# The filter stage of a hybrid diffusion step: sine network in halves, fp32r taps, conditioning tiles and P/Q sums on other engines

## The chip, the cores and the metric

The kernel runs on one core of a Trainium2 chip. The time is the device time of one execution in microseconds (us); the figure that counts is the median of several runs. A core has five engines that run side by side and wait for one another on semaphores: TensorE (PE in the profile; PEld are its weight loads), VectorE (DVE), ScalarE (ACT), GpSimd (POOL) and SyncE (SP), which here only issues DMA transfers. Each engine executes its own instructions in order.

## What is computed

One inference step of a two-layer backbone with 1024 latent and 256 context tokens (`TOK` = 1280) and D = 1024. Layer 0 mixes tokens with a bidirectional long convolution, layer 1 with neighbourhood attention; each is followed by a feed-forward block. The change concerns the filters of layer 0 and the first two of the six conditioning vectors:

```python
def ada_params(cvec, w, b):
    m = (jax.nn.silu(cvec) @ w + b)[:, None, :]
    return jnp.split(m, 6, axis=-1)

def hyena_filters(L, pe_w1, pe_b1, pe_w2, pe_b2, pe_w3, sin_freq, decay):
    ...
    hdn = jnp.sin(sin_freq[0] * (feats @ pe_w1 + pe_b1))
    hdn = jnp.sin(sin_freq[1] * (hdn @ pe_w2 + pe_b2))
    k = (hdn @ pe_w3).astype(jnp.float32) * (jnp.exp(-t * jnp.abs(decay)) + MOD_SHIFT)
    return k[:, :D_MODEL], k[:, D_MODEL:]
```

`bidir_long_conv` then places forward and backward taps on a circle (the backward tap of index 0 is not used) and convolves by a Fourier transform. Everything is float32.

## The kernel before

The filter stage comes first. It has a prologue and forty transforms.

The **sine network** runs over all 1280 tokens at once: TensorE multiplies the 33 position features by `pe_w1` in fp32 into a PSUM tile (L709), VectorE applies bias and frequency and reduces the phase to +-pi in six operations (L527 to L541), ScalarE takes the sine (L454). The second layer (L715, the same six operations, L457) does the same with `pe_w2` and 64 rows. ScalarE then copies the first 128 columns of each token part into `hdb`, and VectorE clears its first column (L544), so that the backward taps of index 0 become zero.

The **taps** are made in 40 groups g: ten blocks of 128 tokens for each of four quarters q of 256 channels. `taps(g)` is two fp32 matmuls of 256 columns (L682, L683) with 64 rows. Meanwhile ScalarE makes the window exp(-t|decay|) (`window`, L423). `generate(g)` on VectorE multiplies both (L553, `ker_ok`) and forms forward + backward and forward - backward, P and Q, with two 256-wide operations (L557, L558, `pq_ok`). ScalarE rounds P/Q to the high part of a split in fp32r (`pq_high`, L432), GpSimd subtracts it for the low part (`pq_low`, L377, `pl_ok`). All of `win`, `pq` and the PSUM banks of the taps have two buffers, so that `window(g)` waits for the sums of g - 2 and `generate(g)` for the low part of g - 2.

A **transform** s = 10 q + j multiplies a slice j of the Fourier basis by ten P/Q blocks: 24 fp32r matmuls of 256 columns for j = 0 to 7, 6 for j = 8 and 9 (L702), into one of three banks. The basis is split like the weights, during quarter 0: ScalarE rounds (`basis_hi`, L413), GpSimd subtracts (`basis_lo`, L372). ScalarE copies the odd half of the bank (`odd_half`, L438), VectorE combines it with the even one into `gout` (`combine`, L567 to L571, `spec_ev`), and SyncE stores it to `spec`. While quarter q is transformed the groups of q + 1 are made: three before the first transform, one before each of the next seven (`made_in`). A transform with j = 0 waits for all ten low parts of its quarter.

The **conditioning**: 16 tiles of 128 outputs times two vectors, on TensorE (`early_tile`, L670: 8 blocks of 128x128 fp32 weights against 2 columns). Four stand between the layers of the sine network, the other twelve in pairs behind tap groups 1 to 6. VectorE adds the bias at transform 20 into `mod`. The later conditioning tiles are made on VectorE, where a tile and a vector take one multiply-and-reduce over 1024 columns (L618, L1948, called a row product below).

In quarter 3 no taps are made. The tiles of x are loaded, modulated and split (`x_high`, L447, `x_low`, L578, L583, L396), and the input projection's first two weight entries are split.

SyncE's queue holds, in this order: the network's inputs, `cvec`, `negt`, `par`, `ident`, the first `w3` and decay, conditioning tiles and basis entries 0 and 1, basis entries 2 to 9 (entry c waits for the split of c - 2), and only then the forty pairs of stores. The Silu of the conditioning rows (`cb`, `crow`) is loaded and made after transform 39 (L496).

Of the kernel before, what the change touches and what calls it, by code (L numbers as in the profile page):

```python
# [49 lines left out]

E_FILT, E_IN, E_FWD, E_INV, E_OUT, E_FFN, E_QKV = 10, 24, 9, 16, 8, 6 * FC, 24


def hyena_natten_step(nc, t):
    ctx = ExitStack()
    with ctx:
# [137 lines left out]
        with stage() as st:  # L194
# [4 lines left out]
            def place(name, at_byte, shape, dt=F32):  # L199
# [8 lines left out]
            adw = [place("ada_early", base_a, [128, 8, 1024]), place("ada_early2", X1 + 8192, [128, 8, 1024])]  # L208
            feats, arg, cyc, hd = [place(n, base_a + 61440 + 5120 * b, [p, TOK])
                                   for b, (n, p) in enumerate((("feats", PE_DIM), ("arg", FILT), ("cyc", FILT), ("hd", FILT)))]  # L210
            win = place("win", base_w + 8192, [128, 2, 2, 256])
            pq = place("pq", base_w + 12288, [128, 2, 2, 256])
            w3 = place("pe_w3", base_w + 16384, [FILT, 2, 2, 256])
            dec = place("dec", base_w + 20480, [128, 2, 2, 256])
            hd2 = place("hd2", REST, [FILT, TOK])
            gout = place("gout", REST + 5120, [128, 4, 2, 256])
            odd = place("odd", REST + 13312, [128, 2, 256])
            hdb = place("hdb", REST + 15360, [FILT, 2, 128])
            negt = place("negt", REST + 16384, [128, 10])
            cvec = place("cvec", REST + 16448, [128, 8, 2])  # L220
            w1 = place("pe_w1", REST + 16512, [PE_DIM, FILT])
            w2 = place("pe_w2", REST + 16768, [FILT, FILT])
            fcol = place("fcol", REST + 17024, [FILT, 4])
# [8 lines left out]
            pt = st.enter_context(nc.psum_tensor("ps_tr", [128, 512], F32))  # L232
            pa = st.enter_context(nc.psum_tensor("ps_ad", [128, 512], F32))
            m_in, c_in, hdb_ok, mlp_mm, arg_ok, dve_s, hd_ok = [
                sem(n, st) for n in ("m_in", "c_in", "hdb_ok", "mlp_mm", "arg_ok", "dve_s", "hd_ok")]
            f_w = [sem(f"f_w{b}", st) for b in range(2)]
            g_out = [sem(f"g_out{b}", st) for b in range(4)]
            ag_in = [sem(f"ag_in{b}", st) for b in range(8)]
            x_in = [sem(f"x_in{k}", st) for k in range(KT)]
            dec_ok, pe_k, win_ok, ker_ok, pq_ok, ph_ok, pl_ok, dft, odd_ok, spec_ev, pe_c, mod_ok = [  # L240
                sem(n, st) for n in ("dec_ok", "pe_k", "win_ok", "ker_ok", "pq_ok", "ph_ok", "pl_ok", "dft", "odd_ok", "spec_ev",
                                 "pe_c", "mod_ok")]
# [9 lines left out]
            ps_mlp = pg[1]  # L252
# [30 lines left out]
            def _(sp):  # L283
                for dst, src in ((feats[:, :], t["feats"]), (w1[:, :], t["pe_w1"]), (w2[:, :], t["pe_w2"]),
                                 (fcol[:, :], t["fcol"])):
                    sp.dma_start(dst, src).then_inc(m_in, 16)
                for dst, src in ((cvec[:, :, :], t["cvec"]), (negt[:, :], t["negt"]), (par[:, :], t["par"]),
                                 (ident[:, :], t["ident"])):
                    sp.dma_start(dst, src).then_inc(c_in, 16)
# [5 lines left out]
                def load_early(b):  # L295
                    sp.dma_start(adw[b // 4][:, 2 * (b % 4):2 * (b % 4) + 2, :],
                                 t["ada"][2 * b:2 * b + 2, :, :].rearrange("a p k -> p a k")).then_inc(ag_in[b], 16)
# [3 lines left out]

                load_gen(0)
                for b in range(4):
                    load_early(b)
                load_entry(sp, 0, wsrc(0))
                load_entry(sp, 1, wsrc(1))
                for b in range(4, 8):
                    load_early(b)
                load_gen(1)
                for j in range(2, 10):  # L310
                    load_entry(sp, j, wsrc(j)[:, 0:basis_width(j)], width=basis_width(j))
                for s in range(40):
                    q, j = s // 10, s % 10
                    if s in (2, 12):
                        sp.wait_ge(pe_k, 10 * q + 10)
                        sp.wait_ge(win_ok, 10 * q + 10)
                        load_gen(q + 2)
# [9 lines left out]
                    for side, tile in enumerate((a, 4 + (a ^ 1)) if j < 8 else (8, 9)):  # L327
                        sp.dma_start(spec[tile, :, j % 2, 256 * q:256 * q + 256], gout[:, s % 4, side, :]).then_inc(g_out[s % 4], 16)
# [3 lines left out]
                for b in range(4):  # L332
                    sp.wait_ge(g_out[b], 320)
# [8 lines left out]
                sp.dma_start(cb[:, :, :], t["crow"]).then_inc(cb_in, 16)  # L342
# [22 lines left out]
            def _(pool):  # L365
# [14 lines left out]
                basis_lo(0)  # L380
                for g in range(10):
                    pq_low(g)
                    if g == 7:
                        basis_lo(1)
                for s in range(30):
                    if s < 8:
                        basis_lo(s + 2)
                    for g in made_in(s):
                        if g % 10:
                            pq_low(g - 1)  # L390
# [16 lines left out]
            def _(act):  # L407
                def basis_hi(j):
                    w = basis_width(j)
                    act.wait_ge(w_loaded[j % 2], 16 * (j // 2) + 16)  # L410
                    if j == 1:
                        act.wait_ge(pe_c, 16)
# [6 lines left out]

                def window(g):  # L420
                    if g >= 2:
                        act.wait_ge(pq_ok, g - 1)
# [3 lines left out]
                def pq_high(g):  # L426
                    act.wait_ge(pq_ok, g + 1)
                    if g == 10:
                        act.wait_ge(pe_c, 16)
# [4 lines left out]
                def odd_half(s):  # L434
# [3 lines left out]
                    act.activation(odd[:, s % 2, :], bank(s)[:, 256:512], ACT.Copy).then_inc(odd_ok, 1)  # L438
# [56 lines left out]
                act.wait_ge(cb_in, 16)  # L495
                act.activation(cb[:, :, :], cb[:, :, :], ACT.Silu).then_inc(cb_ok, 1)  # L496
# [2097 lines left out]
```

## Time and profile before

| | |
|---|---|
| median of 3 runs | 3738.29 us (3730.98 to 3740.62) |
| profiled execution, its own time | 3730.74 us |
| its span, first to last instruction | 3728.9 us |
| TensorE busy | 3552.7 us (95% of the span) |
| VectorE, ScalarE, GpSimd busy | 1519.5, 1033.2, 1231.7 us |
| mean granted TensorE clock | 0.983 |
| filter stage (to the first product of the input projection) | 0 to 252.51 us |

The profiler took one execution. A row of a timeline has the start and duration in us, the engine, the line, the operation, its output and inputs, shapes, and a count where equal neighbours are merged; in brackets stands the idle time before it and what ended it. For merged rows the duration is from the first start to the last end.

### The profile page before, as it was taken

The page shows a single profiled execution, that of the slowest core. Times are in us where ns is not written, and L with a number is a line of the kernel's source. Part 1 is how long each engine was busy: PE and PEld are TensorE (multiplying, and loading weights), DVE is VectorE, ACT ScalarE, POOL GpSimd, SP SyncE. Part 2 cuts the span into 40 slices and gives each one's busy share as a digit, 9 for nine tenths or more (in the row PEclk, how much of TensorE's full clock was granted, in tenths as well). Part 3 has the DMA queues.
Part 4 walks back from the last instruction along what each step waited for, and adds up shares of the span by engine and source line. Part 5 has one row for each costly group of instructions (what it writes and reads, how often), then busy time and mean ns, then how long its engine had stood idle before and what let it go on. Part 6 is the DMA issues. An engine that isn't in the chain of part 4 may idle for free. (4 is left out here: it accounts for less than half of the span.)

```text
span 3728.9 us, 47287 instructions
## 1 busy us (share of the span) xinstructions
PE 3552.7 (95%) x19244; PEld 3067.5 (82%) x19244; DVE 1519.5 (41%) x2472; ACT 1033.2 (28%) x1552; POOL 1231.7 (33%) x813
## 2 busy tenths in 40 slices
PE   8999998989899999999989988999999999999997
PEld 6788887778788888888878877888878888888886
DVE  2775553564434444344451014777340222111116
ACT  1441121232511111111152224777433111111113
POOL 1531112733522222222361203666343222222223
PEclk9999999999999999999999999999999999999998
DMA  3243323754122222222243456777201111111111
GB/s 120 88 168 118 111 87 118 249 186 155 43 68 68 75 73 80 68 63 69 73 155 139 154 171 162 177 176 178 85 29 40 35 40 40 40 35 40 40 40 62
DMA packets 173366, 365.38 MB, mean 98 GB/s; under 512 B 16839, under 2 KB 98247, under 8 KB 171496
## 3 DMA queue, kind: packets, MB, share of 16 engines
q1 hardware_dynamic: 167720, 352.01, 29.9%
q10 hardware_dynamic: 5440, 10.49, 0.9%
q8 instruction: 146, 2.39, 0.3%
q14 instruction: 60, 0.49, 0.0%
HBM read 284.84 MB, written 77.59 MB: 97 GB/s over the span
## 5 line engine op out<-in xcount | busy, mean ns | idle before, releaser
L148 POOL TENSOR_TENSOR w_lo<-w_raw,w_hi 128x1024 fp32r<-128x1024 f32 x207 | 504.0, 2435 | 1438.6 <-ACT w_hi L142 1438.3
L156 PE MATMUL ps_r<-a_hi,w_hi 128*128 128x512 f32 (+1 forms) x2496 | 888.4, 356 | 19.8 <-POOL a_lo L1813 11.6
L156 PE MATMUL ps_r<-a_lo,w_hi 128*128 128x512 f32 (+1 forms) x2496 | 884.7, 354 | 0.0
L156 PE MATMUL ps_r<-a_hi,w_lo 128*128 128x512 f32 (+1 forms) x2496 | 883.5, 354 | 0.0
L156 PEld LDWEIGHTS ps_r<-a_hi,w_hi 128*128 128x128 f32 x2496 | 472.8, 189 | 97.1 <-POOL a_lo L1813 19.8
L156 PEld LDWEIGHTS ps_r<-a_hi,w_lo 128*128 128x128 f32 x2496 | 472.4, 189 | 65.8
L156 PEld LDWEIGHTS ps_r<-a_lo,w_hi 128*128 128x128 f32 x2496 | 472.8, 189 | 65.2 <-issue 1.0
L142 ACT ACTIVATE w_hi<-w_raw 128x1024 fp32r<-128x1024 f32 x207 | 217.6, 1051 | 955.3 <-PE ps_r L156 555.6
L2012 DVE TENSOR_TENSOR hid_l<-hid_l,ps_r 128x1280 f32<-128x1280 f32 x44 | 65.5, 1488 | 824.5 <-PE ps_r L156 824.5
L2032 DVE SCALAR_TENSOR_TENSOR x_t_l<-ps_r,mod,x_t_l 128x1024 f32<-128x1024 f32 (+1 forms) x288 | 241.4, 880 | 260.3 <-PE ps_r L156 260.3
L156 PE MATMUL ps_in<-x_split_f,w_hi 128*128 128x512 f32 (+1 forms) x1152 | 310.5, 358 | 2.1 <-DVE gout_f L571 2.1
L156 PE MATMUL ps_r<-hid_lo_l,w_hi 128*128 128x512 f32 (+1 forms) x864 | 307.3, 356 | 0.0
L156 PE MATMUL ps_r<-hid_hi_l,w_hi 128*128 128x512 f32 (+1 forms) x864 | 306.7, 355 | 0.0
L156 PE MATMUL ps_r<-hid_hi_l,w_lo 128*128 128x512 f32 (+1 forms) x864 | 305.6, 354 | 0.0
L1853 POOL TENSOR_TENSOR hid_lo_l<-hid_l,hid_hi_l 128x1280 fp32r<-128x1280 f32 x42 | 134.5, 3201 | 481.2 <-ACT hid_hi_l L1751 481.2
L1948 DVE CUSTOM_DVE_ANT_0 ps_x<-ada_w_l,silu_c_l 128x1024 f32<-128x1024 f32 x116 | 198.7, 1713 | 110.4 <-DMA ada_w_l<-in_ada_t 107.8
L156 PEld LDWEIGHTS ps_in<-x_split_f,w_hi 128*128 128x128 f32 x1152 | 206.0, 191 | 32.7 <-DVE gout_f L571 2.3
L156 PE MATMUL ps_in<-x_split_f,w_lo 128*128 128x512 f32 (+1 forms) x576 | 204.9, 356 | 0.0
L1751 ACT ACTIVATE hid_hi_l<-hid_l 128x1280 fp32r<-128x1280 f32 x44 | 56.1, 1274 | 534.2 <-DVE hid_l L2012 534.2
L156 PEld LDWEIGHTS ps_r<-hid_hi_l,w_hi 128*128 128x128 f32 x864 | 163.4, 189 | 24.4
L156 PEld LDWEIGHTS ps_r<-hid_hi_l,w_lo 128*128 128x128 f32 x864 | 162.9, 189 | 23.6
L156 PEld LDWEIGHTS ps_r<-hid_lo_l,w_hi 128*128 128x128 f32 x864 | 163.4, 189 | 22.7
(254 smaller groups left out, 6023.0 us busy)
## 6 DMA issues: line engine op xcount, KB each, us to landing
w_raw<-in_w_all SPq DMA_DIRECT2D x213, 512.0 KB, 3.5
ada_w_l<-in_ada_t SPq DMA_DIRECT2D x59, 512.0 KB, 3.5
v_hl<-v_d SPq DMA_DIRECT2D x128, 128.0 KB, 2.9
t_tail_f<-in_ada_t SPq DMA_DIRECT2D x24, 512.0 KB, 4.2
spec<-gout_f SPq DMA_DIRECT2D x80, 128.0 KB, 2.1
g_spec_c<-spec ACTq DMA_DIRECT2D x20, 512.0 KB, 5.2
v_d<-z_v_l SPq DMA_DIRECT2D x10, 1024.0 KB, 4.3
q_hl_l<-q_d SPq DMA_DIRECT2D x32, 320.0 KB, 7.3
```

Source lines behind the costliest of these rows:

```text
L142: act.activation(wh[:, s, 0:width], raw[:, s, 0:width], ACT.Copy).then_inc(w_hi, 1)
L148: pool.tensor_tensor(wl[:, s, 0:width], raw[:, s, 0:width], wh[:, s, 0:width].bitcast(F32), ALU.subtract).then_inc(w_split, 1)
L156: last = pe.matmul(out[:, c0:c1], w[:, c % 2, blk * 128:blk * 128 + 128], x[:, c0:c1], start=start and b == 0 and term == 0, stop=stop and ...
L1751: act.activation(hh[:, i % 2, k, :], sg[:, :], ACT.Copy).then_inc(hh_ok, 1)
L1853: pool.tensor_tensor(hl[:, i % 2, k, :], sg[:, :], hh[:, i % 2, k, :].bitcast(F32), ALU.subtract).then_inc(hl_ok, 1)
L1948: dve.tensor_tensor_reduce(out=px[:, :], in0=w[:, :], in1=vec[:, q, :], scale=1.0, scalar=0.0, op0=ALU.mult, op1=ALU.add, accum_out=acc_a[ ...
L2012: dve.tensor_tensor(sg[:, :], sg[:, :], pg[1][:, 0:TOK], ALU.mult).then_inc(gated, 1)
L2032: ins = dve.scalar_tensor_tensor(xt[:, m, p0:p1], pg[m % 2][:, p0:p1], gate[:, p:p + 1], xt[:, m, p0:p1], ALU.mult, ALU.add)
```

## The change

- **Sine network in halves.** Tokens 0 to 639 and 640 to 1279 go through `hidden`, `phase` and `sine` one after the other, in their own PSUM tiles. `pe_w2` is doubled to 128 columns, so the second layer's values stand in both halves of the partitions; its result is split there into a high part (rounded in all 128 rows) and a low part in rows 64 to 127 (`hidden_low` on GpSimd). The conditioning tiles are cut in halves (`early_part`), three of them before the second half of layer 2.
- **Taps.** `w3` is split too, high and low (`w3_high`, `w3_low`), in both halves of the rows. `taps(g)` is four fp32r matmuls of 256 columns with 128 rows: the split hidden values times the high and the low part. The unused backward tap is now cleared behind the product, by a memset of one partition in groups 0 and 8 of each quarter. `hdb` goes.
- **Conditioning.** Seven tiles stay on TensorE (`E_PE`), with tiles 2 to 6 in halves behind the first ten tap groups. Nine go to VectorE: 18 row products (`early_row`) at transforms 9 to 26 with a PSUM tile as scratch; their 512 KB each are loaded between the stores. `mod` is made at transform 27, and the next two weight entries are loaded after transform 28.
- **P/Q sums.** For groups 20 to 39 GpSimd makes both 256-wide sums (`pq_make`).
- **Loads and buffers.** The order of the first loads is new, and basis entries 4 to 9 are loaded one by one behind the stores of transforms 0 to 5. `gout` has two buffers instead of four. The conditioning rows are loaded at the start and their Silu is made between the sines of layer 2.

```diff
+E_PE = 7
+PQ_DVE = 20
...
+def load_early(m):
+    sp.dma_start(adw[:, m, :], t["ada"][m, :, :]).then_inc(ag_in[m], 16)
+def load_row(n):
+    sp.dma_start(raw[:, n % 2, :], t["ada_e"][n, :, :]).then_inc(er_in[n % 2], 16)
...
 for s in range(40):
...
+    if s == 8:
+        sp.wait_ge(w_split, 10)
+        load_row(0)
+        load_row(1)
+    if s > 9 and s in ROWS_AT and s % 2 == 0 and s // 2 - 3 < 16 - E_PE:
+        sp.wait_ge(er_ok, s - 8)
+        load_row(s // 2 - 3)
...
     sp.wait_ge(spec_ev, 1 + s + 1)
...
-    if s == 20:
+    if s < 6:
+        load_entry(sp, s + 4, wsrc(s + 4)[:, 0:basis_width(s + 4)], width=basis_width(s + 4))
+    if s == 28:
+        sp.wait_ge(er_ok, 2 * (16 - E_PE))
         load_entry(sp, ei, wsrc(ei))
         load_entry(sp, ei + 1, wsrc(ei + 1))
...
+def pq_make(g):
+    if g < PQ_DVE:
+        return
+    pool.wait_ge(ker_ok, g + 1)
+    pool.wait_ge(pl_ok, g - 1)
+    pool.tensor_tensor(pq[:, g % 2, 0, :], win[:, g % 2, 0, :], win[:, g % 2, 1, :], ALU.add)
+    pool.tensor_tensor(pq[:, g % 2, 1, :], win[:, g % 2, 0, :], win[:, g % 2, 1, :],
+                       ALU.subtract).then_inc(pq_p, 1)
...
+w3_low(0)
+pool.wait_ge(w3_ok, 1)
+hidden_low(0)
+hidden_low(1)
+pool.wait_ge(hs_ok, 2)
 for g in range(10):
     pq_low(g)
-    if g == 7:
-        basis_lo(1)
+    if g in (1, 7):
+        basis_lo(g // 7)
+    if g == 4:
+        w3_low(1)
...
+sine(0, 0)
+sine(0, 1)
+w3_high(0)
+sine(1, 0)
+act.wait_ge(cb_in, 16)
+act.activation(cb[:, :, :], cb[:, :, :], ACT.Silu).then_inc(cb_ok, 1)
+sine(1, 1)
...
+def early_row(n):
+    r, q = n // 2, n % 2
...
+    dve.tensor_tensor_reduce(out=pta[:, :], in0=raw[:, r % 2, :], in1=cb[:, q, :], scale=1.0, scalar=0.0,
+                             op0=ALU.mult, op1=ALU.add, accum_out=acc_e[:, r, q:q + 1]).then_inc(er_ok, 1)
...
     for g in made_in(s):
         generate(g)
+    if s in ROWS_AT:
+        early_row(s - ROWS_AT[0])
...
     combine(s)
...
-    fwd = hd2[:, n * 128:n * 128 + 128]
-    bwd = hdb[:, n // 8, :] if n in (0, 8) else fwd
-    pe.matmul(gbank(g)[:, 0:256], fwd, w3[:, q % 2, 0, :], start=True, stop=True)
-    pe.matmul(gbank(g)[:, 256:512], bwd, w3[:, q % 2, 1, :], start=True, stop=True).then_inc(pe_k, 1)
+    for way in range(2):
+        for term, w in enumerate((w3h, w3l)):
+            last = pe.matmul(gbank(g)[:, 256 * way:256 * way + 256], hs[:, n * 128:n * 128 + 128],
+                             w[q % 2][:, way, :], start=term == 0, stop=term == 1)
+    last.then_inc(pe_k, 1)
...
+hidden(0, 0)
+hidden(0, 1)
+early_part(0, 0)
+hidden(1, 0)
+early_part(0, 1)
+early_part(1, 0)
+hidden(1, 1)
+early_part(1, 1)
 for g in range(10):
     taps(g)
-    if 1 <= g <= 6:
-        early_tile(2 * g + 2)
-        early_tile(2 * g + 3)
+    early_part(2 + g // 2, g % 2)
```

## Rows read from the trace of the kernel before

**Rows 1.** Windows by stage: for each engine busy us (count), then granted clock.
```profile
41.24:110.56 69.32, 64.03 (x241) 55.15 (x239) 22.26 (x35) 16.21 (x26) 17.90 (x12) 1.00 0.04 9
110.56:152.80 42.24, 38.63 (x246) 33.52 (x245) 32.75 (x50) 21.22 (x39) 27.24 (x17) 0.99 0.39 126
152.80:191.01 38.21, 37.66 (x245) 32.91 (x244) 28.72 (x50) 15.78 (x32) 13.23 (x10) 0.96 0.22 77
191.01:224.70 33.69, 33.55 (x234) 29.71 (x234) 26.13 (x48) 13.88 (x28) 13.22 (x10) 1.00 0.26 90
224.70:252.51 27.81, 24.87 (x204) 24.46 (x204) 20.28 (x36) 15.56 (x26) 12.04 (x5) 1.00 0.86 292
```

**Rows 2.** Timeline of the prologue: start, us, engine, line, what, count.
```profile
4.18 4.53 PE L709 MATMUL ps_in<-feats_f,pe_w_f 33*64 33x512 f32 x6 [4.18 <-DMA fcol_f<-in_fcol]
...
29.61 1.60 DVE L527 TENSOR_SCALAR arg_f<-ps_in,fcol_f 64x1280 f32<-64x1280 f32 x1 [13.59 <-PE ps_in L715]
...
36.84 1.27 ACT L457 ACTIVATE hd_f<-arg_f 64x1280 f32<-64x1280 f32 x1 [15.84 <-DVE arg_f L541]
...
41.24 0.69 DVE L553 SCALAR_TENSOR_TENSOR win_f<-win_f,ps_in 128x512 f32<-128x512 f32 x1 [2.47 <-ACT win_f L423]
...
42.53 6.98 PE L670 MATMUL ps_ad<-silc,ada_early_f 128*128 128x2 f32 x32
...
49.45 1.22 PE L682 MATMUL ps_in<-pe_w_f,hd_f 64*128 64x256 f32 x2
```

**Rows 3.** Waits, first 250 us: us in total, times, longest.
```profile
DVE win_f L553 <- PE ps_in L683: 43.7, 7, 7.4
```

**Rows 4.** Timeline around the first two transforms, all engines.
```profile
105.64 1.27 POOL L377 TENSOR_TENSOR pq_lo_f<-pq_f,pq_hi_f 128x512 fp32r<-128x512 f32 x1 [1.02 <-ACT pq_hi_f L432]
...
110.56 0.58 PE L702 MATMUL ps_in<-pq_hi_f,basis_f 128*128 128x256 f32 x1
110.58 1.46 POOL L377 TENSOR_TENSOR pq_lo_f<-pq_f,pq_hi_f 128x512 fp32r<-128x512 f32 x1 [1.36 <-ACT pq_hi_f L432]
...
113.06 1.45 POOL L377 TENSOR_TENSOR pq_lo_f<-pq_f,pq_hi_f 128x512 fp32r<-128x512 f32 x1 [1.02 <-ACT pq_hi_f L432]
...
115.42 0.70 PE L682 MATMUL ps_in<-pe_w_f,hd_f 64*128 64x256 f32 x2
...
116.47 0.39 PE L702 MATMUL ps_in<-pq_hi_f,basis_f 128*128 128x256 f32 x1
...
119.53 0.70 PE L682 MATMUL ps_in<-pe_w_f,hd_f 64*128 64x256 f32 x2
```

**Rows 5.** Timeline of VectorE in quarter 0.
```profile
118.22 1.41 DVE L557 TENSOR_TENSOR pq_f<-win_f 128x256 f32<-128x256 f32 x1
...
139.16 0.42 DVE L567 TENSOR_TENSOR gout_f<-ps_in,odd_f 128x256 f32<-128x256 f32 x1 [5.75 <-DMA spec<-gout_f]
```

**Rows 6.** Timeline: row products of a later stage beside a GpSimd weight split.
```profile
1299.17 1.23 DVE L1948 CUSTOM_DVE_ANT_0 ps_x<-ada_w_l,silu_c_l 128x1024 f32<-128x1024 f32 x1 [3.57 <-DMA ada_w_l<-in_ada_t]
...
1299.48 3.17 POOL L148 TENSOR_TENSOR w_lo<-w_raw,w_hi 128x1024 fp32r<-128x1024 f32 x1 [12.46 <-ACT w_hi L142]
...
1300.50 3.25 DVE L1948 CUSTOM_DVE_ANT_0 ps_x<-ada_w_l,silu_c_l 128x1024 f32<-128x1024 f32 x1
```

**Rows 7.** Groups by line and shape, GpSimd, whole run: busy us, mean ns, idle.
```profile
L372 POOL TENSOR_TENSOR basis_f<-w_raw,basis_f 128x1024 fp32r<-128x1024 f32 x8 | 19.3, 2408 | 23.7 <-ACT basis_f L413 23.7
L1805 POOL TENSOR_TENSOR sum_x_l<-sum_x_l,x_t_l 128x256 f32<-128x256 f32 x24 | 17.7, 737 | 5.0 <-DVE x_t_l L1887 3.6
```

**Rows 8.** DMA issues, first 250 us: count, KB each, median us to landing.
```profile
w_raw<-in_w_all SPq DMA_DIRECT2D x10, 512.0 KB, 3.8
```

**Rows 9.** Groups by line and shape, filter stage.
```profile
L423 ACT ACTIVATE win_f<-dec_f,negt_f 128x512 f32<-128x512 f32 x40 | 28.1, 711 | 0.1
...
L413 ACT ACTIVATE basis_f<-w_raw 128x1024 fp32r<-128x1024 f32 x8 | 8.4, 1049 | 2.6 <-DMA w_raw<-in_w_all 2.6
```

**Rows 10.** Timeline of ScalarE in quarter 3.
```profile
232.57 1.74 ACT L447 ACTIVATE x_split_f<-x_raw_f,aff 128x1024 fp32r<-128x1024 f32 x2 [1.55 <-DMA x_raw_f<-in_x]
```

More of the change, by code:

```diff
@@ new lines, in hyena_natten_step @@
+            w1 = place("pe_w1", base_a + 25600, [PE_DIM, FILT])
+            w2 = place("pe_w2", base_a + 26112, [FILT, 128])
+            adw = place("ada_early", base_a + 26624, [128, E_PE, 1024])
+            gaps = [base_a + 66560 + 4096 * n for n in range(4)]
+            w3h, w3l = [[place(f"{n}{b}", gaps[2 * v + b], [128, 2, 256], F32R) for b in range(2)]
+                        for v, n in enumerate(("w3_hi", "w3_lo"))]
+            odd = [place(f"odd{b}", gaps[b] + 2048, [128, 256]) for b in range(2)]
@@ L218, in hyena_natten_step @@
[L218 to L223, printed above, removed]
+            hs = place("hd_split", REST, [128, TOK], F32R)
+            gout = place("gout", REST + 5120, [128, 2, 2, 256])
+            negt = place("negt", REST + 9216, [128, 10])
@@ L545, in _ @@
+                for layer in range(2):
+                    for h in range(2):
+                        phase(layer, h)
                 dve.sem_inc(spec_ev, 1)
@@ L663, in _, with early_part, hidden @@
             def _(pe):
-                def early_tile(m):
-                    if m == 0:
-                        pe.wait_ge(hd_ok, 1)
-                    w = adw[m // 8][:, m % 8, :]
-                    pe.wait_ge(ag_in[m // 2], 16)
-                    for k in range(8):
-                        last = pe.matmul(pa[:, 2 * m:2 * m + 2], w[:, k * 128:k * 128 + 128], silc[:, k, :],
-                                         start=k == 0, stop=k == 7)
-                    last.then_inc(pe_c, 1)
+                def early_part(m, h):
+                    if m == 0 and h == 0:
+                        pe.wait_ge(silc_ok, 1)
+                    if h == 0:
+                        pe.wait_ge(ag_in[m], 16)
+                    for k in range(4 * h, 4 * h + 4):
+                        last = pe.matmul(pe_ad[:, 2 * m:2 * m + 2], adw[:, m, k * 128:k * 128 + 128], silc[:, k, :],
+                                         start=k == 0, stop=k == 7)
+                    if h:
+                        last.then_inc(pe_c, 1)
+                def hidden(layer, h):
+                    if layer:
+                        pe.wait_ge(sin_ok, h + 1)
+                    t0 = HALVES[h][0]
+                    for c0, c1 in ((0, 512), (512, 640)):
+                        if layer == 0:
+                            last = pe.matmul(ps_mlp[h][0:FILT, c0:c1], w1[:, :], feats[:, t0 + c0:t0 + c1], start=True, stop=True)
+                        else:
+                            last = pe.matmul(ps_mlp[h][:, c0:c1], w2[:, :], hd[:, t0 + c0:t0 + c1], start=True, stop=True)
+                    last.then_inc(mlp_mm, 1)
                 def taps(g):
```

248 lines of the change are left out of this document (146 added, 102 removed).

## The prediction

> **What bounds the kernel now.** I read the windows by stage first. The change touches only the filter stage, the first 252.5 us of 3728.9; the rest keeps its code and only moves earlier [rows 1]. The stage is a prologue (sine network and the taps of quarter 0, up to the first transform at 110.56) and four quarters of ten transforms. These begin at 110.56, 152.80, 191.01 and 224.70, and the first product of the next stage at 252.51: 42.2, 38.2, 33.7 and 27.8 us.
>
> The timeline then says what each waits for. In the prologue after 41.24 TensorE is busy 64.0 of 69.3 us [rows 1], but with a pair of conditioning tiles (6.98 us) between two tap groups [rows 2]; VectorE waits 43.7 us for taps [rows 3]. In the quarters TensorE is the clock: taps start at 115.42 and 119.53, a pitch of 4.11, of which the transform from 116.47 has 3.06 and the taps 1.05 [rows 4]. A low part takes GpSimd 1.27 to 1.46 of it [rows 4].
>
> Then I looked at pairs of GpSimd and VectorE rows. A 256-wide sum takes VectorE 0.42 where GpSimd rests, 1.41 where it works [rows 5]. The 1024-wide row product took 1.23, but 3.25 while GpSimd split weights, and that split 3.17 instead of 2.41 [rows 6, 7]. Operations with two SBUF inputs and GpSimd's thus take turns. Nothing in quarters 1 and 2 uses that up now, with GpSimd busy 13.2 us in each [rows 1]. The change does.
>
> **Part 1, sine network.** A 1280-wide layer takes VectorE 7.23 us (29.61 to the sine at 36.84) in six operations. A 512-wide product takes 0.69 and a 256-wide sum 0.42, so about 0.15 of each is fixed [rows 2, 5]: half a layer is (7.23 - 0.9) / 2 + 0.9, with the gaps 4.2. TensorE's 4.53 per layer [rows 2] gives 2.27 per half, and half a conditioning tile is a quarter of 6.98, 1.75. TensorE starts at 4.2 as before; layer 1 is on VectorE from 6.55 to 14.95. The second layer's first half ends on TensorE at 13.9, its phases run 14.95 to 19.15. The other half goes behind three half tiles, ends at 19.7, and its phases at 23.95. From there to the first kernel product it was 4.40 (36.84 to 41.24); less half a sine and the two copies, plus a rounding, 4.2. The first product comes at 28.15 for 41.24: **-13.1**. The Silu of the conditioning rows lies between the two sines, where ScalarE waits for VectorE; late data for it would add up to 2. Four conditioning tiles in front of layer 2 go, and the copies with the cleared tap, whose work is now a memset of one partition behind two products per quarter, which I take at 0.2 each.
>
> **Part 2, first ten tap groups.** From the first product at 41.24 to the tenth low part at 105.64 it was 64.4 us, six groups of it at 8.9 (6.98 and the taps). Now TensorE needs per group four fp32r matmuls of 256 columns at 0.217 in its slow state (twice the 0.118 of part 3; the two-column ones, which are no faster, take 6.98 / 32 = 0.218 [rows 2]) = 0.87, and one half tile, 1.72: 2.59. The other engines' loop, where TensorE isn't in the way, is the pitch of the low parts at 110.58 and 113.06, 2.48 [rows 4]. So the two are nearly equal. Into GpSimd's loop come two basis splits (2.41 each) and one of w3 (1.27, by size a low part). A loop has 2.48 - 1.27 = 1.2 idle, so they cost about 1.2 + 1.2 + 0.1, and with turns 2.9. From the first product: 2.4 to its low part, 9 x 2.48, 2.9 and the memset 0.2 = 27.8 for 64.4: **-36.6**. Bounds: 25 with the splits hidden, 33 with each at full price. From the tenth low part to transform 0 it was 4.92, and the taps ahead of it are 0.8 shorter: **-0.8**. Transform 0 at 60.0, **-50.5** in all; bounds -45 and -55. Loads don't bind: what must have landed by 28 us is under 7 MB, 24 us at quarter 3's 292 GB/s [rows 1]; late tiles count as the upper bound.
>
> **Part 3, quarter 0.** The 24 matmuls of transform 1 take 3.06 with the way in and out [rows 4], 24 x 0.118 = 2.83 without. The fp32 taps take 0.85, the fp32r ones 0.47, and the two changes between them 0.43 today (4.11 - 2.83 - 0.85), which I take as 0.28: 3.58 if TensorE alone decided. But GpSimd needs 2.41 + 1.27 + two turns of 0.2, about 4.1 with its wake-up, and VectorE's two sums wait for both. The basis entries 4 to 7 are now loaded only behind the stores of transforms 0 to 3: two store issues 1.0, load 3.8 [rows 8], rounding 1.05, window 0.71 [rows 9], P/Q high and odd half 1.0, combination 0.84 = 8.4 per two transforms, 4.2 each. So five transforms stay at 4.1, two fall to 3.6. What goes is the wait for stores that stood behind seven weight loads in SyncE's queue: 5.75 us of VectorE at 139.16 [rows 5]. Together 38.3 for 42.2: **-3.9**; bounds 36 and 42. Two gout buffers for four cost nothing as long as a store (about 3 us with its issue) lands within two transforms; at 3.6 each there are 4 us to spare.
>
> **Part 4, quarters 1 and 2.** TensorE alone would give 8 x 3.58 + 1.5 (two short ones) + 3.1 (the three tap groups between quarters) = 33.2 for 38.2, and 30.3 for 33.7. But GpSimd now makes the sums. No such row stands in this stage; the nearest, a 256-wide addition elsewhere, is 0.74 [rows 7], 0.70 from start to start. A group costs GpSimd 2 x 0.70 + 1.22 = 2.62, and each row product holds it off by about 1.07 (its 1.23 less the fixed part). Quarter 1: ten groups 26.2 + eight turns 8.6 = 34.8, counted from 0.6 before its first transform. The last P/Q high stands ahead of transform 17's odd half in ScalarE's queue, and two low parts follow its sum: 34.2 - 2.4 + 0.9 for these two, 0.7 for the combination = 33.4. Behind that on VectorE are two row products at 1.3 with turns of 1 and 0.5, two combinations and the product of group 30 (5.8 in all), which releases the last taps (0.7): 39.9 for 38.2, **+1.7**. Quarter 2 has seven row products and no such tail: 26.2 + 7.5 - 0.6 = 33.1 for 33.7, **-0.6**. Bounds 33.2 to 42 and 30.3 to 36. What fp32r and the gaps save on TensorE, 0.53 x 30 = 16 us, is mostly hidden behind GpSimd.
>
> The Trainium skill warns of this: "Perfetto Trace Analysis", section "Optimizing Scalar/DVE Operations", says that GpSimd and VectorE share a read port, so that moving work from one to the other might not help. The trace agrees (3.25 us for 1.23). By the rule taken plainly quarters 1 and 2 would change by 0 and the total be 3678; by my sum they change by +1.1.
>
> **Part 5, quarter 3.** The next two weight entries load after transform 28 instead of 20: 1 MB just ahead of the x tiles, for whose first one ScalarE already waits till 232.57, 7.9 after the quarter began [rows 10]. 1 MB at 292 GB/s [rows 1] is 3.6 us, partly overlapped, and ScalarE's rounding of the entries waits in front of two odd halves: **+1.5**, bounds 0 and 4. The Silu and load of the rows leave the next stage, where ScalarE idled: 0.
>
> **Sum.** -50.5 - 3.9 + 1.7 - 0.6 + 1.5 = **-51.8** against the profiled execution's own 3730.7 (its span of 3728.9 and 1.8 around it): 3679. The median of the runs is 7.6 higher, which gives 3686. I say 3684.
>
> **Rivals.** A, TensorE keeps the beat: turns overlap better than counted and the quarters take 36, 33.2, 30.3 and 27.8: 50.5 + 6.2 + 5.0 + 3.4 = -65, 3670. For it: GpSimd's 13.2 busy of 38.2 and 33.7 leave room [rows 1]. Against: 34.8 us of GpSimd work and turns. B, every turn costs full price: prologue -45, quarters 0, +3.8, +2.3, +4: -35, 3700. For it: 3.25 for 1.23. Against: in the quarters now a sum waits for at most one GpSimd operation. C, the other side: TensorE stays at its low clock. The granted clock reads 1.00 in the prologue and in quarter 2 [rows 1], but a tap pair took 1.22 in the first and 0.70 in the quarters [rows 2, 4]: that is 1.2 and 2.4 GHz. Transform 0, after a prologue of two-column tiles and a wait, took 4.86 to the next taps, transform 1 3.06. If the new waits held it low, 24 x 0.096 x 32 = 74, with the short transforms 78: +26, 3757. It decides once two thirds of the transforms run low. Against: by the plan TensorE waits under 1 us at a time within a quarter. That the change doesn't do what it says is half my forecast already: the taps get shorter, the quarters don't.
>
> **Numbers.** Forecast 0.62 (3674 to 3694), A 0.18, B 0.17, C 0.02, other 0.01. The range 3665 to 3704 takes in A, B and the bounds. A measurement here tells 0.3% (11 us) from no change. All but C gain over 30: faster 0.97, same 0.01, slower 0.02.
>
> **What would show it.** First kernel product near 28, first transform near 60, low parts of the prologue 2.5 apart; GpSimd over 70% busy in quarter 1, VectorE's row products stretched, the quarter not under 37. Wrong if row products and sums take no turns (quarters of 33 and 30), if low parts come 3.5 apart, or if transforms in the quarters take over 4.

## The result, and the profile after

The changed kernel takes 3697.48 us (median of 4 runs, 3692.15 to 3700.8) beside 3735.17 for the kernel before in the same session (4 runs, 3730.98 to 3740.62). The ratio is 0.9897, with a 95% interval of 0.9877 to 0.9916: about 38 us or 1.0% faster. The forecast was 3684, the range 3665 to 3704. The profiled execution took 3700.8, its span is 3698.9.

The windows by stage of the changed kernel answer to [rows 1], with the prologue cut at the first kernel product (columns: window and length; busy us and count of PE, PEld, DVE, ACT, POOL; granted clock, DMA share, GB/s):

```profile
0.00:29.87 29.87, 21.79 (x72) 16.18 (x72) 18.32 (x24) 10.79 (x14) 4.97 (x9) 1.00 0.64 243
29.87:63.17 33.30, 24.20 (x108) 23.53 (x109) 29.69 (x37) 17.08 (x27) 22.73 (x14) 1.00 0.09 32
63.17:113.74 50.57, 35.99 (x246) 34.07 (x246) 36.08 (x53) 21.89 (x39) 29.66 (x20) 0.87 0.42 130
113.74:153.45 39.71, 33.00 (x245) 32.50 (x245) 30.69 (x52) 17.03 (x32) 35.68 (x32) 0.89 0.48 146
153.45:186.88 33.43, 28.97 (x234) 28.79 (x233) 24.57 (x45) 14.61 (x28) 32.14 (x29) 0.96 0.28 88
186.88:220.54 33.66, 26.74 (x204) 25.93 (x205) 17.58 (x35) 16.68 (x26) 13.21 (x5) 0.91 0.80 274
```

Transform 0 starts at 63.17 for 110.56, which is 47.4 us won. The four quarters last 50.6, 39.7, 33.4 and 33.7 us for 42.2, 38.2, 33.7 and 27.8: 15.4 us are given back, 8.3 of them in quarter 0 and 5.9 in quarter 3. What follows the first product of the next stage (220.54) takes 3478.4 us, 3476.4 before, so the case is decided in the filter stage. By this first product (called X below) the gain is 32.0 us; the medians give 38, since the profiled execution before (3730.74) was faster than each of its four runs and the changed one (3700.8) is the slowest of its four.

**Where quarter 0 went.** The waits of this window (engine and line, what it waits for: us in total, times, longest) show entries of the basis that come late, and then what holds up the taps of the next quarter: the split of `w3`, a product of VectorE, and in front of that product a row's load:

```profile
ACT basis_f L476 <- DMA w_raw<-in_w_all: 15.3, 6, 3.6
...
PE ps_in L805 <- POOL w_lo_f L426: 4.6, 1, 4.6
PE ps_in L805 <- DVE win_f L640: 4.5, 1, 4.5
DVE ps_tr L660 <- DMA w_raw<-in_ada_e: 4.4, 1, 4.4
```

The timeline gives the ring behind the first of these. SyncE's queue, then ScalarE and VectorE:

```profile
74.93 0.46 SPq L134 DMA_DIRECT2D w_raw<-in_w_all  x1
...
85.23 0.79 SPq L361 DMA_DIRECT2D spec<-gout_f  x2
86.07 0.46 SPq L134 DMA_DIRECT2D w_raw<-in_w_all  x1
```
```profile
79.31 1.06 ACT L476 ACTIVATE basis_f<-w_raw 128x1024 fp32r<-128x1024 f32 x1 [3.14 <-DMA w_raw<-in_w_all]
80.28 0.71 ACT L492 ACTIVATE win_f<-dec_f,negt_f 128x512 f32<-128x512 f32 x1
```
```profile
81.02 0.69 DVE L642 SCALAR_TENSOR_TENSOR win_f<-win_f,ps_in 128x512 f32<-128x512 f32 x1 [1.37 <-ACT win_f L492]
81.74 1.37 DVE L648 TENSOR_TENSOR pq_f<-win_f 128x256 f32<-128x256 f32 x1
83.03 1.50 DVE L649 TENSOR_TENSOR pq_f<-win_f 128x256 f32<-128x256 f32 x1
84.46 0.41 DVE L669 TENSOR_TENSOR gout_f<-ps_in,odd_f 128x256 f32<-128x256 f32 x1
```

An entry issued at 74.93 can be rounded at 79.31. The window stands behind the rounding on ScalarE. On VectorE its product and both sums (3.4 us, each sum stretched from 0.42 by a GpSimd operation) stand in front of the combination at 84.46. Behind that come the store at 85.23 and the load two entries later at 86.07. From load to load the ring takes 11.1 us for two transforms (10.6 to 11.1 in its four rounds); the forecast had 8.4. Transforms 0 to 3 took 15.1 us, the three behind them, which wait for late entries, 15.7, and the last three with the taps of the next quarter 19.9.

The end of quarter 0 on VectorE: the row product waits for its load, and the combination of transform 9 and the product of group 20 stand behind it.

```profile
109.79 1.23 DVE L660 CUSTOM_DVE_ANT_0 ps_tr<-w_raw,silu_c_f 128x1024 f32<-128x1024 f32 x1 [4.36 <-DMA w_raw<-in_ada_e]
110.94 0.14 DVE L660 DVE_READ_ACCUMULATOR2_ANT ada_acc_e_f<- 128x1 f32 x1
110.94 0.42 DVE L669 TENSOR_TENSOR gout_f<-ps_in,odd_f 128x256 f32<-128x256 f32 x1
111.28 0.41 DVE L673 SCALAR_TENSOR_TENSOR gout_f<-ps_in,odd_f 128x256 f32<-128x256 f32 x1
111.61 0.68 DVE L638 SCALAR_TENSOR_TENSOR win_f<-win_f,ps_in 128x512 f32<-128x512 f32 x1
```

On TensorE this is the second of two waits in the timeline, the first being for the split of `w3` for quarter 2:

```profile
106.13 0.58 PE L805 MATMUL ps_in<-w_hi_f,hd_split_f 128*128 128x256 f32 x1 [4.55 <-POOL w_lo_f L426]
...
112.72 0.58 PE L805 MATMUL ps_in<-w_hi_f,hd_split_f 128*128 128x256 f32 x1 [4.51 <-DVE win_f L640]
```

**Quarters 1 and 2.** The groups by line and shape in 113.7 to 187 us, GpSimd and then VectorE (busy us, mean ns of one, idle before), show the turns:

```profile
L412 POOL TENSOR_TENSOR pq_lo_f<-pq_f,pq_hi_f 128x512 fp32r<-128x512 f32 x20 | 29.7, 1488 | 0.0
L420 POOL TENSOR_TENSOR pq_f<-win_f 128x256 f32<-128x256 f32 x19 | 22.1, 1165 | 5.2 <-DVE win_f L640 2.8 <-DVE win_f L642 0.2
```
```profile
L660 DVE CUSTOM_DVE_ANT_0 ps_tr<-w_raw,silu_c_f 128x1024 f32<-128x1024 f32 x17 | 29.2, 1715 | 0.0
```

GpSimd is busy 35.7 of 39.7 and 32.1 of 33.4 us. A first sum takes 1.17 instead of the 0.73 it has alone (below), a row product 1.72 instead of 1.23. One meeting in the timelines of both engines:

```profile
137.50 1.30 POOL L412 TENSOR_TENSOR pq_lo_f<-pq_f,pq_hi_f 128x512 fp32r<-128x512 f32 x1
...
137.82 2.06 DVE L660 CUSTOM_DVE_ANT_0 ps_tr<-w_raw,silu_c_f 128x1024 f32<-128x1024 f32 x1
...
138.94 1.54 POOL L420 TENSOR_TENSOR pq_f<-win_f 128x256 f32<-128x256 f32 x1
```

TensorE meanwhile ran its transforms 3.36 apart, and waited 6.05 for the split of `w3` before the taps of group 30.

**Quarter 3.** Its waits:

```profile
DVE gout_f L669 <- DMA spec<-gout_f: 8.8, 5, 3.0
...
ACT w_hi L144 <- DMA w_raw<-in_w_all: 6.3, 1, 6.3
DVE gout_f L669 <- ACT odd_f L507: 5.4, 2, 5.0
```

VectorE has two `gout` buffers, and waits in five transforms for a store that is still under way while the tiles of x are loaded. In this window half of the stores land within 2.4 us, but one takes 7.2. In the same quarter of the kernel before the longest took 9.0, and with four buffers VectorE waited for none.

### The profile page after: what moved, and what is told of

Same layout as the page of the kernel before. It is cut to its first block and busy times, and to the rows that moved or that the text cites. A ratio compares the mean times of both kernels' runs of the same rounds, so it can differ in the third digit from the quotient of the medians.

```text
span 3698.9 us, 47103 instructions
## 1 busy us (share of the span) xinstructions
PE 3501.8 (95%) x19104; PEld 3037.1 (82%) x19104; DVE 1528.8 (41%) x2488; ACT 1037.8 (28%) x1558; POOL 1283.8 (35%) x859
## 5 line engine op out<-in xcount | busy, mean ns | idle before, releaser
L158 PEld LDWEIGHTS ps_in<-x_split_f,w_hi 128*128 128x128 f32 x1152 | 206.7, 192 | 35.7 <-DVE gout_f L673 5.0
```

The lines of the kernel that those rows point to most:

```text
L158: last = pe.matmul(out[:, c0:c1], w[:, c % 2, blk * 128:blk * 128 + 128], x[:, c0:c1], start=start and b == 0 and term == 0, stop=stop and ...
```

## The experiments

The first product of the next stage (X, at 220.54 in the changed kernel) is the measure, since what follows it took 3471 to 3482 us in these traces with the same code. Each experiment was run once, the two versions four times. Lengths in us, from the starts of transforms 0, 10, 20 and 30 in each trace:

| kernel | T0 | q0 | q1 | q2 | q3 | X |
|---|---|---|---|---|---|---|
| before | 110.56 | 42.2 | 38.2 | 33.7 | 27.8 | 252.51 |
| changed | 63.17 | 50.6 | 39.7 | 33.4 | 33.7 | 220.54 |
| loads first | 62.94 | 44.8 | 39.8 | 33.4 | 33.5 | 214.44 |
| entries at 26 | 63.02 | 51.1 | 39.6 | 33.4 | 33.9 | 221.01 |
| w3 split early | 63.02 | 50.9 | 40.9 | 33.6 | 33.5 | 221.92 |
| rows two later | 62.92 | 47.1 | 39.2 | 34.1 | 35.0 | 218.25 |
| sums on VectorE | 63.16 | 50.8 | 36.4 | 30.8 | 34.3 | 215.43 |
| taps twice | 63.14 | 51.2 | 41.1 | 32.4 | 35.2 | 222.94 |
| short rows | 63.08 | 49.7 | 36.1 | 30.5 | 33.6 | 213.04 |
| three gouts | 63.03 | 50.2 | 40.2 | 33.1 | 31.4 | 217.88 |
| more conditioning | 69.97 | 51.3 | 39.7 | 33.4 | 33.2 | 227.61 |
| version 1 | 63.01 | 43.3 | 36.5 | 30.8 | 32.0 | 205.52 |
| version 2 | 63.03 | 38.9 | 34.0 | 34.4 | 32.1 | 202.47 |

**Basis loads ahead of the stores.** The load of entry s + 4 goes in front of SyncE's wait for the combination of s.

```diff
+if s < 6:
+    load_entry(sp, s + 4, wsrc(s + 4)[:, 0:basis_width(s + 4)], width=basis_width(s + 4))
 sp.wait_ge(spec_ev, 1 + s + 1)
...
-if s < 6:
-    load_entry(sp, s + 4, wsrc(s + 4)[:, 0:basis_width(s + 4)], width=basis_width(s + 4))
```

> One line moved: SyncE issues the load of basis entry s + 4 ahead of its wait for the combination of transform s, not behind its stores; nothing is left out. Quarter 0 took 50.6 us in the changed kernel and 38.3 was forecast. Theory L (the loads behind the stores set the pace of transforms 4 to 9 and, through the last entries, the late end of the quarter): quarter 0 falls to 40 to 44. Rival G (GpSimd's basis splits and low parts, in turns with VectorE's sums, set the pace): it stays above 47. Both: quarters 1 and 2 stay within 1 us of 39.7 and 33.4.

Quarter 0 fell by 5.8 us to 44.8, the run took 3692.39. Its waits for entries fell from 15.3 us to:

```profile
ACT basis_f L476 <- DMA w_raw<-in_w_all: 3.0, 2, 2.9
```

The ring is real, and worth 5.8 us, a little less than the 6.6 to 10.6 expected; the rest of the 12 us stays. The start of transform 7 moved from 93.89 to 89.12, but from there to transform 10 it still took 18.6 us (19.9 in the changed kernel).

**Row products two transforms later.** All rows and their loads move, so that none stands ahead of the combination of transform 9.

```diff
-ROWS_AT = range(9, 9 + 2 * (16 - E_PE))
+ROWS_AT = range(11, 11 + 2 * (16 - E_PE))
...
-        sp.wait_ge(er_ok, s - 8)
-        load_row(s // 2 - 3)
+        sp.wait_ge(er_ok, s - 10)
+        load_row(s // 2 - 4)
```

> The 18 row products go to transforms 11 to 28 instead of 9 to 26, with their loads moved alike; nothing is left out. In the changed kernel VectorE stood 4.4 us in front of the first row product, with the combination of transform 9 and the product of group 20 behind it. Theory R (that wait is on the path to transform 10): quarter 0 loses 4 to 6 us, to 45 to 47, and quarter 3 gains 1 to 3, since the modulation comes two transforms later. Rival: quarter 0 stays above 49, because low parts and w3 split hold transform 10 as long.

Quarter 0 fell by 3.5, half a us less than the 4 to 6 expected, and quarter 3 grew by 1.4; the run took 3693.98. In place of the 4.36 us wait the combination of transform 9 now waits for a store (VectorE's timeline):

```profile
107.21 0.42 DVE L669 TENSOR_TENSOR gout_f<-ps_in,odd_f 128x256 f32<-128x256 f32 x1 [1.95 <-DMA spec<-gout_f]
107.55 0.41 DVE L673 SCALAR_TENSOR_TENSOR gout_f<-ps_in,odd_f 128x256 f32<-128x256 f32 x1
107.88 0.68 DVE L638 SCALAR_TENSOR_TENSOR win_f<-win_f,ps_in 128x512 f32<-128x512 f32 x1
```

The product of group 20 comes at 107.88 for 111.61, which accounts for the quarter's gain.

**Split of w3 two transforms earlier**, on ScalarE and GpSimd.

```diff
-if s in (8, 18):
+if s in (6, 16):
```

> Only the place of the w3 splits for quarters 2 and 3 in ScalarE's and GpSimd's queues is changed, from transforms 8 and 18 to 6 and 16; nothing is left out. TensorE waited 4.6 and 6.1 us for them ahead of tap groups 20 and 30. Theory W (that wait is part of the path): quarters 0 and 1 each lose 2 to 5 us. Rival S (the products of groups 20 and 30 come late anyway, behind row products and combinations on VectorE, and TensorE only waits there instead): both stay within 1 us of 50.6 and 39.7.

The wait for the split is gone and the time is not: the two waits of TensorE became one, quarter 1 even grew by 1.2 us, and the run took 3706.07.

```profile
PE ps_in L805 <- DVE win_f L640: 9.8, 1, 9.8
```

So the row's load ended last at this boundary. In version 2 below, without a row there, the wait for the split is what is left: it was next in line.

**P/Q sums back on VectorE.**

```diff
-PQ_DVE = 20
+PQ_DVE = 40
```

> The P/Q sums of groups 20 to 39 go back to VectorE, all else as changed; nothing is left out. Quarters 1 and 2 took 39.7 and 33.4 us in the changed kernel. Theory G (GpSimd's chain of ten sums and ten low parts, 26.2 us, plus the turns it takes with the row products sets quarters 1 and 2): GpSimd is freed of 14 us a quarter, VectorE carries 10 x (0.72 + 0.70 + 0.67 + 1.3) = 34 plus some turns, and they take 35 to 38 and 30.5 to 33. Rival V (VectorE would have been the bound without the move, so the move was needed): they take over 41 and over 34.5.

Quarters 1 and 2 fell by 3.3 and 2.7, the run took 3696.23. The windows by stage (columns as above):

```profile
113.92:150.32 36.40, 31.57 (x246) 31.15 (x245) 35.85 (x73) 16.41 (x33) 15.70 (x11) 0.92 0.53 159
150.32:181.09 30.77, 29.80 (x234) 29.63 (x233) 29.80 (x64) 13.65 (x28) 13.22 (x10) 0.93 0.31 96
```

GpSimd drops from 35.7 to 15.7 us in quarter 1, and VectorE becomes the bound, with 35.9 of 36.4 us busy. The move of the sums to GpSimd costs this change 6.0 us in the two quarters, 5.1 at X.

**Row products over 64 columns for 1024.** This leaves out most of the sum for nine of the sixteen conditioning tiles.

```diff
-out=pta[:, :], in0=raw[:, r % 2, :], in1=cb[:, q, :],
+out=pta[:, 0:64], in0=raw[:, r % 2, 0:64], in1=cb[:, q, 0:64],
```

> The 18 row products read 64 of their 1024 columns (their loads stay whole); what they leave out is most of the sum of nine conditioning tiles. It takes their time on VectorE and their turns with GpSimd away, and keeps every wait. Theory G: quarter 1 loses eight turns of 1.07 us and the two products at its end, 39.7 to 28 to 32 (then near TensorE's 30 with 3.36 per transform), quarter 2 seven turns, 33.4 to 27 to 29. Rival (GpSimd's own 26.2 us and the queue order of ScalarE set them, turns are covered): both lose under 3 us. Quarter 0 loses 1.3, as its wait for the load stays.

Quarters 1 and 2 fell by 3.6 and 2.9 (run 3689.44). The groups in 112.8 to 179.5 us:

```profile
L412 POOL TENSOR_TENSOR pq_lo_f<-pq_f,pq_hi_f 128x512 fp32r<-128x512 f32 x20 | 25.7, 1291 | 0.0
...
L420 POOL TENSOR_TENSOR pq_f<-win_f 128x256 f32<-128x256 f32 x19 | 14.0, 734 | 12.8 <-DVE win_f L642 7.8 <-DVE win_f L640 4.8
```

A low part is 0.20 and a first sum 0.43 shorter, and GpSimd now idles 12.8 us for 5.2 before its sums. With GpSimd freed quarter 1 ends at TensorE's own work, 8 x 3.36 + 1.5 + 3.1 = 31.5 by the forecast's way of counting, plus its waits for the split of `w3` (2.4) and the product of group 30 (0.5) and a first transform at the lower clock (4.8 for 3.1). These were not in the 28 to 32 and 27 to 29 expected: both quarters came out above, and near the rival's bound of 3 us. The turns are shown, since the same GpSimd instructions got shorter, but of the 14 us that they take only 6.5 came back as time.

**Taps twice from group 20 on.** The four matmuls are done two times.

```diff
-for way in range(2):
+for way in (0, 1, 0, 1) if g >= 20 else (0, 1):
```

> TensorE makes the taps of groups 20 to 39 twice (the same four fp32r matmuls again, the second set overwriting the first); the result is unchanged. That is 0.47 us of TensorE more per group, 4.7 per quarter, about what the fp32 taps cost more. Theory G (TensorE waits for GpSimd about 6 us ahead of tap groups 20 and 30, so its taps are covered): quarters 1 and 2 change by less than 1 us. Rival T (TensorE's time counts): each grows by 4 to 5 us, to 44 and 38.

TensorE got four matmuls of 0.12 more per group, 4.8 us per quarter. Quarter 1 rose by 1.4 and quarter 2 fell by 1.1, each a little more than the 1 us expected and far from the rival's 4 to 5; the run took 3702.72. The timeline of GpSimd, with transforms now 3.84 apart, shows that it now waits a little for its input in each group:

```profile
132.18 1.66 POOL L420 TENSOR_TENSOR pq_f<-win_f 128x256 f32<-128x256 f32 x1 [0.18 <-DVE win_f L642]
...
136.02 1.66 POOL L420 TENSOR_TENSOR pq_f<-win_f 128x256 f32<-128x256 f32 x1 [0.24 <-DVE win_f L642]
```

So TensorE had 0.3 us per transform to spare (3.64 between GpSimd's groups at 131.67 and 135.31 in the changed kernel, 3.36 on TensorE): what fp32r saves there is mostly hidden in the quarters, as forecast. Why quarter 2 came out shorter is not settled; its window has a granted clock of 1.00, for 0.96.

**Weight entries before quarter 3** are loaded at transform 26 instead of 28.

```diff
-if s == 28:
+if s == 26:
```

> One number changed: the two weight entries of the next stage are loaded behind transform 26 instead of 28; nothing is left out. Quarter 3 took 33.7 us in the changed kernel, 27.8 before. Theory E (ScalarE stands 6.3 us in front of the first entry, and the x tiles queue behind both): quarter 3 falls to 28 to 30. Rival (ScalarE and VectorE work on x sets the length, only started late by the combinations that GpSimd delays): it stays above 32.

Quarter 3 stayed at 33.9 (run 3693.97) for the 28 to 30 expected. ScalarE's wait of 6.3 us for the entries is gone, and the wait for `gout` grew:

```profile
DVE gout_f L669 <- DMA spec<-gout_f: 9.8, 6, 4.3
```

The test is not clean: transform 30 ran at a granted clock of 0.50 in this run (first 5.7 us of the quarter; 0.75 in the changed kernel) and its matmuls were out about 0.7 us later, counted from its start.

**A third gout buffer** in free space, with s % 3 in its stores and waits.

```diff
-dve.wait_ge(g_out[s % 2], 32 * (s // 2))
+dve.wait_ge(g_out[s % 3], 32 * (s // 3))
```

> gout gets a third buffer; nothing is left out. In quarter 3 of the changed kernel VectorE waits 8.8 us in five pieces for stores out of gout, which stand behind 2.5 MB of x in the DMA rings; in the kernel before, with four, none there. Quarter 3 took 33.7, 27.8 before. Theory D (two buffers are the main cause): quarter 3 falls by 2.5 to 4.5, to 29 to 31; the other 2 to 2.5 us are transform 30 at the low clock after TensorE's wait. Rival E (the late x tiles set the length and the waits only fill it): it falls by less than 1. Quarters 0 to 2 unchanged in both.

Quarter 3 fell by 2.3 (run 3695.73), a little under what was expected. The wait for stores is off the top of its list, where now stand:

```profile
DVE gout_f L670 <- ACT odd_f L508: 7.0, 2, 6.5
...
ACT w_hi L144 <- DMA w_raw<-in_w_all: 5.9, 1, 5.9
```

With the store out of the way the entries come last: ScalarE holds the odd half of transform 30 behind them. The two waits lie side by side, which fits that loading the entries earlier gave nothing by itself; both remedies together were not tried.

**More conditioning in the prologue.** Each of the ten half tiles behind the tap groups is multiplied twice, into a scratch column.

```diff
 early_part(2 + g // 2, g % 2)
+for k in range(4 * (g % 2), 4 * (g % 2) + 4):
+    pe.matmul(pe_ad2, adw[:, 2 + g // 2, k * 128:k * 128 + 128], silc[:, k, :], start=True, stop=True)
```

> Behind each of the first ten tap groups TensorE makes its half conditioning tile a second time, into a bank that nobody reads: 10 x 1.72 us of two-column matmuls added, as if twelve tiles had stayed on TensorE, in halves; nothing is left out. Transform 0 began at 63.2 in the changed kernel. Theory P (the prologue's gain comes from TensorE's conditioning work leaving the space between tap groups, until its 2.6 us per group match the other engines' 2.5 to 2.9): the pitch becomes 4.3 and transform 0 begins 12 to 16 us later, at 75 to 79. Rival (cutting the tiles in halves and the fp32r taps made the gain, by letting engines overlap): less than 6 us later.

TensorE got about 17 us more work (ten half tiles of 1.7), and transform 0 came 6.8 us later, between the two expectations: half of what theory P said, a little more than the rival (run 3708.08). The window from the first product to transform 0:

```profile
29.87:69.97 40.10, 39.59 (x185) 39.30 (x186) 20.39 (x37) 16.97 (x27) 21.55 (x14) 1.00 0.09 27
```

TensorE is full at 4.27 us per group here; in the changed kernel it is busy 24.2 of 33.3 us, and the loop over the other engines sets the pace. There TensorE is through with its ten groups at 51.75, 11.4 us before transform 0, so 17 us more can cost only a part of themselves. From first product to transform 0 it is 69.3 us before, 40.1 here and 33.3 in the changed kernel: the five tiles that are moved back here account for 6.8 of the 36 us won. Two more tiles moved (7.0 of TensorE), taps of 1.0 instead of 2.0 per group, and halves instead of pairs of tiles between them share the other 29, and no run separates these.

**Version 1: loads first, three gouts, sums on VectorE.**

> Three edits together: basis loads ahead of the stores, three gout buffers, P/Q sums back on VectorE; nothing is left out. If they add up, quarters of 45, 36.4, 30.8 and 31.5 after a prologue of 63 put the first product at 207 in place of 220.5: 13 us less than the changed kernel, about 3684. Rival (they overlap, as the gout waits move when quarter 3 starts earlier): 6 to 9 us.

It takes 3686.74 us (median of 4), 0.9879 of the kernel before with an interval of 0.9861 to 0.9898. X is 205.5 for the 207 expected, 15.0 before the changed kernel's; the three alone add up to 13.9 (6.1, 5.1 and 2.7). Between the medians it is 10.7.

**Version 2: version 1 with the rows placed by hand**, none at the transforms 9, 18 and 19, each loaded when its buffer comes free.

```diff
-ROWS_AT = range(9, 9 + 2 * (16 - E_PE))
+ROWS_AT = (*range(10, 18), 20, 20, 21, 22, 22, *range(23, 28))
...
+for r in range(2, 16 - E_PE):
+    if ROWS_AT[2 * r - 3] == s:
+        sp.wait_ge(er_ok, 2 * r - 2)
+        load_row(r)
```

> The same three edits, and the 18 row products at transforms 10 to 17 and 20 to 27 (two of them in 20 and in 22), none at 9, 18 and 19, where they stand in front of the product that releases the last taps of a quarter; nothing is left out. Theory R (those three places are on the path): quarter 0 loses 4 to 5 us and quarter 1 2 to 3 beyond v1, 3677 in all. Rival (row products moved into quarter 2 lengthen it as much): as v1 within 2 us.

It takes 3680.95 us (median of 4, 3679.06 to 3681.98), 0.9860 of the kernel before (0.9842 to 0.9878): the fastest of all, for the 3677 expected. Its median is 16.5 us below the changed kernel's, its X 18.1. The windows of its quarters:

```profile
63.03:101.97 38.94, 32.59 (x246) 31.75 (x246) 34.86 (x53) 22.37 (x40) 29.41 (x18) 0.93 0.46 146
101.97:135.97 34.00, 30.97 (x245) 30.48 (x245) 32.28 (x69) 16.64 (x33) 15.58 (x11) 0.95 0.60 180
135.97:170.33 34.36, 29.00 (x234) 28.42 (x233) 33.84 (x67) 14.00 (x28) 15.26 (x10) 0.95 0.33 103
170.33:202.47 32.14, 27.05 (x204) 26.51 (x204) 21.69 (x39) 17.23 (x27) 13.58 (x5) 0.92 0.83 292
```

Quarters 0 and 1 gain 4.4 and 2.4 over version 1, as theory R had it: TensorE's wait of 4.7 us for the product of group 20 in version 1 is gone, its wait of 4.2 for the split of `w3` stays. The rows crowded into quarter 2 fill VectorE (33.8 of 34.4) and take 3.6 back, as the rival had it, so that X gains 3.1 in all. Quarter 0 is now within 0.6 us of the 38.3 that were forecast.

## Why the prediction was right in sign and range, and 14 us off in size

The medians differ by 38 us where 52 were summed. At X, where the parts are counted, it is 32.0 for 51.8: 20 us short, and 6 of the 20 don't show in the medians, by luck of which executions were profiled. All parts that failed failed the same way, so nothing cancelled; the range held because it was wide enough. By its own parts:

- **Part 1, sine network: right, 1.7 short.** First kernel product 29.87 for 28.15. The missing term is a turn: the split of `w3` (GpSimd, 16.41 to 17.68) and that of the hidden values (21.96 to 23.68) each hold up one VectorE phase operation, which take 1.57 and 2.04 for 0.49 and 0.82. The first of the two reads one SBUF tile only, so turns are not confined to operations with two SBUF inputs, as the forecast had it.
- **Part 2, ten tap groups: right, 3.2 late together with part 1.** Tenth low part 28.98 behind the first product for 27.8, transform 0 at 63.17 for 60.0. Between splits the low parts stand 2.5 apart, as said, and more TensorE work moved the end by only 6.8 of 17 us. Together the prologue won 47.4 of 50.5. (The matmul at the lower clock, 0.217, was called twice 0.118, which is 0.236; measured are 0.21 and 0.12.)
- **Part 3, quarter 0: wrong by 12.3, the step that failed.** Forecast 38.3, came 50.6. Two of its terms failed. The first is the ring "8.4 per two transforms": it had 1.0 for P/Q high and odd half between window and combination, and left out that VectorE's queue has a product and two stretched sums there (3.4); the load itself took 4.4 for 3.8; it is 11.1. Loads first gave 5.8 back. The second is the end of the quarter, which the forecast took as three tap groups that nothing holds up. From transform 7 to transform 10 it counted 10.6 us and it took 19.9. There the first row's load, issued at 105.51 behind stores, lands at 109.8, and the split of `w3` has to follow the last low part of quarter 1. Rows two later gave 3.5, the rows placed by hand 4.4 on top of version 1, whose quarter 0 of 43.3 has the loads first and the third buffer. The forecast has no term for the row product in quarter 0, costed the others as VectorE time alone, and asked of their loads nothing.
- **Part 4, quarters 1 and 2: right.** 39.7 and 33.4 for 39.9 and 33.1. GpSimd's own work plus turns is the bound, as summed: in the two quarters the turns on it are 20 x 0.20 + 19 x 0.43 + 20 x 0.05 and 1.0 of a `w3` split (2.26 for 1.28) = 14 us, 0.8 per row product, where 8.6 + 7.5 were taken at 1.07; its groups stood 3.64 apart. Of the two ways to relieve it, sums on VectorE gave 6.0 us and short rows 6.5, and more TensorE work cost 0.3 in all. The Trainium skill, "SBUF — State Buffer", section "SBUF: two separate sides", says that GpSimd and a VectorE operation with two SBUF inputs take the shared port pair as a lock for a whole instruction. The trace agrees: a row product that starts at 137.82 beside a low part of 137.50 to 138.80 takes 2.06 us, its 1.23 and most of what was left of the low part, and the sum that starts at 138.94 takes 1.54 for 0.73.
- **TensorE's own pitch: mis-sized, without effect.** 3.58 was forecast, 3.36 measured. The "two changes" between fp32 taps and transforms, 0.43 in [rows 4] and taken as 0.28, are gone once the taps are fp32r: 24 x 0.12 + 4 x 0.12 = 3.36.
- **Part 5, quarter 3: wrong by 4.4, and for another reason.** Forecast 29.3, came 33.7. "Two gout buffers for four cost nothing" failed: it had 4 us to spare at a store of about 3, but in quarter 3, with loads of x that keep the DMA share at 0.80, the longest store takes 7.2, and VectorE waits 8.8 us. The third buffer gave 2.3 back. Loading the entries earlier, which the forecast's 1.5 hung on, gave nothing with two buffers. The clock is not the rest: TensorE waits 4.46 us ahead of transform 30, whose first matmuls are then 0.21 apart as in the prologue, the later ones 0.12, but version 1 ran that transform at a granted clock of 1.00 and version 2 its start at 0.62, and the quarter took 32.0 and 32.1. What is left in these two, 4.2 us over the kernel before, stays open. They moved 9.38 MB in the quarter at 292 to 294 GB/s, the kernel before 8.12 MB at 292; the 1.26 MB more, most of it the two entries, would take 4.3 at that rate. That is an estimate that fits; the run that would test it, three buffers with the entries loaded earlier, was not made.
- **The rivals.** A (TensorE keeps the beat) fell on GpSimd's 35.7 busy us. B gave 3700 and names the time better than the forecast (-35 at X, where -32.0 came), but by luck: the turns that it charged in full were no dearer than forecast, quarters 1 and 2 took +1.5 and -0.3 for its +3.8 and +2.3, and the largest loss, 8.3 in quarter 0, sat where it had 0. C did not come, though the granted clock of quarters 0 and 1 fell to 0.87 and 0.89 through the waits at their ends: the first transform of quarter 1 takes 4.8 us to its taps (113.74 to 118.5), the second 2.9.

## What to carry to other kernels

When a load is moved behind a store, follow the whole ring from its issue back to its issue, with every instruction that stands in each engine's queue between, and not just the links the semaphores name: here a product and two sums made 8.4 into 11.1. When work leaves one engine for another, ask what the first instruction at the new place waits for, and what stands behind it: a row product of 1.2 us held the next quarter's taps for 4.5 because its load came late. And before a buffer count is cut, take the longest landing of the stage where the DMA engines are busiest, not a typical one: the kernel before already had a store of 9.0 us in quarter 3.

## What the runs showed that was not expected

- A memset of one partition with 256 columns took 0.27 us on VectorE, more than half of a whole 128 x 256 sum (0.42).
- Groups of fp32r taps with 128 rows between fp32r transforms leave no gap on TensorE (3.36 us for 28 matmuls of 0.12); with the fp32 taps of 64 rows a group took 0.43 beyond the matmuls' own time. Whether type or rows make the difference no run separates.
- A VectorE operation with one SBUF input (`tensor_scalar`, 128 x 640) took 1.57 us for its 0.49 beside a GpSimd subtraction.
- TensorE was busy 39.6 of 40.1 us in the run with more conditioning, at a granted clock that reads 1.00, and its fp32r matmuls of 256 columns were 0.21 us apart all that time (0.12 in the quarters): 1.2 GHz, not 2.4. The column is not to be read as the fast level there; the spacing of equal matmuls tells it.
